# Decoder step on one core: key, mask and value steps of the sample attention moved into the projections

## The reference

```python
hn = _rmsnorm(x, g_pre_mix)
xl, gate, q, k, v, qi, ki, wi = _split_proj(hn @ w_in)
# rope on q, k, qi, ki
lru, hT, new_buf = _rglru(xl, conv_buf, h0, ...)        # conv, gates, linear recurrence
att = attend(q, k, v, qi, ki, wi)
mix = concat([lru * gelu(gate), att]) @ w_out
x = x + _rmsnorm(mix, g_post_mix)
f = square(relu(_rmsnorm(x, g_pre_ffn) @ w_ff1)) @ w_ff2
x = x + _rmsnorm(f, g_post_ffn)
```

```python
sc = _index_scores(qi, wi, ki_all)                       # admissible keys only
_, idx = lax.top_k(sc, kk)
s = einsum('...thd,...tkhd->...thk', q, kg) * HEAD_DIM ** -0.5
o = einsum('...thk,...tkhd->...thd', softmax(s), vg)
```

## Time and profile before

| | us |
|---|---|
| median of 3 runs | 909.92 |
| profiled execution | 904.44 |
| its span | 902.2 |
| TensorE busy | 821.2 |
| VectorE / ScalarE / GpSimd busy | 393.9 / 347.7 / 178.0 |

### The profile page before, as it was taken

How to read it: one execution, slowest core, us unless ns; L and a number is a source line. 1 busy time by engine, 2 the same in 40 slices (tenths; PEclk the granted TensorE clock), 3 DMA queues, 4 the chain that set the end, 5 groups by cost and what they waited for, 6 DMA issues and landing times.

```text
span 902.2 us, 16225 instructions
## 1 busy us (share of the span) xinstructions
PE 821.2 (91%) x6089; PEld 673.2 (75%) x6089; DVE 393.9 (44%) x762; ACT 347.7 (39%) x744; POOL 178.0 (20%) x173
## 2 busy tenths in 40 slices
PE   5997799899999888989996999999999999999990
PEld 4863487677865442336884899999999999999990
DVE  6129999993000342430188544322211443333327
ACT  3556455255555452422252434322222343322210
POOL 0731073433243500000023211100000111100003
PEclk9999999989999887997998999999999999999995
DMA  8421325767669869990011222222222222222202
GB/s 343 160 94 49 138 93 188 281 236 257 233 198 309 278 249 388 386 396 35 1 48 47 70 78 84 93 94 90 74 93 94 77 87 93 78 89 91 93 23 99
DMA packets 52179, 133.20 MB, mean 148 GB/s; under 512 B 6113, under 2 KB 6626, under 8 KB 50850
## 3 DMA queue, kind: packets, MB, share of 16 engines
q1 hardware_dynamic: 49442, 113.08, 36.1%
q10 hardware_dynamic: 864, 10.58, 3.3%
q0 software_dynamic: 1824, 8.86, 2.5%
HBM read 127.84 MB, written 4.67 MB: 147 GB/s over the span
## 4 chain that ended last, share of the span: by engine, by line
PE 76%; DVE 6%; DMA 6%; SPq 4%; ACT 3%; issue 3%; POOL 1%; DVEq 0%; ACTq 0%
PE bank L1571 41%; PE bank L1277 21%; SPq L372 3%; PE bank L1388 3%; PE bank L1426 3%; DMA arena<-in_ck 2%; DMA arena<-in_cv 2%; DMA wring<-in_cv 1%; PE bank L1476 1%; PE bank L1263 1%; PE bank L1400 1%; DVE scp L1015 1%; PE bank L1360 1%; DVE lx L951 1%; DVE lx L1195 1%
## 5 line engine op out<-in xcount | busy, mean ns | idle before, releaser
L1277 PE MATMUL bank<-regR,wring 128*128 128x272 f32 x640 | 155.6, 404 | 6.4 <-ACT lx L585 3.2
L1277 PEld LDWEIGHTS bank<-regR,wring 128*128 128x128 f32 x640 | 124.1, 195 | 34.9 <-issue 5.3
L1205 DVE TENSOR_TENSOR h_lo<-lx,h_hi 128x544 f32 (+1 forms) x32 | 35.8, 1120 | 111.0 <-ACT h_hi L865 110.8
L535 POOL TENSOR_TENSOR lx<-lx 128x544 f32<-128x544 f32 x30 | 32.8, 1093 | 244.6 <-ACT lx L860 244.6
L1571 PE MATMUL bank<-h_lo,w_hi_odd 128*128 128x272 f32 x256 | 73.9, 289 | 0.0
L1571 PE MATMUL bank<-h_hi,w_hi_even 128*128 128x272 f32 x256 | 73.8, 288 | 0.0
L1571 PE MATMUL bank<-h_lo,w_hi_even 128*128 128x272 f32 x256 | 73.7, 288 | 0.0
L1571 PE MATMUL bank<-h_hi,w_hi_odd 128*128 128x272 f32 x256 | 73.7, 288 | 0.0
L1571 PE MATMUL bank<-h_hi,w_lo_odd 128*128 128x272 f32 x256 | 73.6, 287 | 0.0
L1571 PE MATMUL bank<-h_hi,w_lo_even 128*128 128x272 f32 x256 | 73.5, 287 | 0.0
L1571 PE MATMUL bank<-hn_lo,w_hi_odd 128*128 128x272 f32 x240 | 69.3, 289 | 0.0
(11 more groups left out here) (267 smaller groups left out, 1711.2 us busy)
## 6 DMA issues: line engine op xcount, KB each, us to landing
arena<-in_ck SPq DMA_DIRECT2D x128, 256.0 KB, 3.8
wring<-in_w_mlp SPq DMA_DIRECT2D x64, 512.0 KB, 3.4
arena<-in_cv SPq DMA_DIRECT2D x80, 256.0 KB, 6.3
wring<-in_cv SPq DMA_DIRECT2D x48, 256.0 KB, 6.4
wring<-in_w_in ACTq DMA_DIRECT2D x4, 2048.0 KB, 8.5
wring<-in_w_in SPq DMA_DIRECT2D x2, 2048.0 KB, 12.9
regX<-in_xT SPq DMA_DIRECT2D x4, 544.0 KB, 5.5
regX<-in_xT POOLq DMA_DIRECT2D x1, 2176.0 KB, 11.6
```

What stands on the lines that cost most here:

```text
L535: nc.gpsimd.tensor_tensor(square_t[:, s, :], relu_t[:, s, :], relu_t[:, s, :], ALU.mult).then_inc(h_sq, 1)
L1205: vec.tensor_tensor(h_lo[:, at], square_t[:, parity, :], h_hi[:, at].bitcast(F32), ALU.subtract).then_inc(h_lo_rd, 1)
L1277: ins = pe.matmul(bank[e % 4][0:parts, 0:HALF], lhs(k), rhs[:, k, hf * HALF:(hf + 1) * HALF], start=(k == 0), stop=(k == KT - 1))
```

## The change

- `K_UNIT = 4`: four key steps stand behind each of the four tiles of k and of xl, none behind gate and v. The ring of key pages keeps its three slots.
- The new keys' scores and the ten mask products stand among the halves of the gate tiles, as do the first five groups of transposes; the others, and 14 value steps (`MID_VALUES`), stand among the v tiles. The remaining 18 value steps stand in the loop over prompt units, one in each second turn.
- Banks 4 and 5 take the mask products, the sample's transposes and value sums; the prompt's scores go to banks 2 and 3.
- The transposed numerators get other homes (the place of the indexer queries, of the index scores and of `kw_diag`), since regR still holds the normed input. Values have three slots (`V_SLOTS`), not five, and the first weight slot is free earlier: its output block is loaded by ScalarE behind the last gate tile.
- VectorE makes the masks before the scans of blocks 1 to 3.

```diff
-V_SLOTS = 5
+V_SLOTS = 3
+K_UNIT = 4
+MID_VALUES = 14
...
-            for s in range(3, V_SLOTS):
-                values(s, s, gemm_mm, E_V)
             for s in (30, 31):
                 keys(s, (s + 2) % 3, k_mm, s - 2)
             for s in range(3):
                 values(s, s, k_mm, KSTEPS - 2 + s)
-            with eng.Fori(0, 5) as i:
+            with eng.Fori(0, 9) as i:
...
-                for i in range(2):
-                    key_scores(8 + 2 * unit + i)
+                if unit < 4:
+                    for i in range(K_UNIT):
+                        key_scores(16 + K_UNIT * unit + i)
+                if between:
+                    between()
...
+            for j in range(2):
+                value_tile(j)
+                sample_transposes(5 + 2 * j)
+                value_products(3 * j)
+                sample_transposes(6 + 2 * j)
+                value_products(3 * j + 1)
+                value_products(3 * j + 2)
...
-            for u in range(KSTEPS + 5):
+            for u in range(ATT_UNITS + 5):
                 if u < ATT_UNITS and u % 2 == 0:
                     att_scores(u // 2)
-                if u < 10:
-                    sample_transposes(u)
...
-                if u >= 5:
-                    value_products(u - 5)
+                if u % 2 == 1 and MID_VALUES + u // 2 < KSTEPS:
+                    value_products(MID_VALUES + u // 2)
```

More of the change, by code:

```diff
@@ L1110, in _ @@
                 vec.tensor_scalar(sstat[:, g, 6:7], sstat[:, g, 5:6], -1.0, None, ALU.mult).then_inc(smax_rd, 1)
+            for c in range(1, CT):
+                scan(c)
             def masked(u):
@@ L1401, in lru_gate, with unit_end @@
                           start=True, stop=True).then_inc(lg_mm, 1)
-            def unit_end(unit):
+            def unit_end(unit, between=None):
                 gates = unit >= 0 and unit % 3 == 1
@@ L1432, in _, with new_key_scores @@
-            for g in range(GRP):
-                eng.wait_ge(k_ev, KSTEPS)
[L1434 to L1450, removed]
+            def new_key_scores():
+                eng.wait_ge(rope_out, 13)
+                eng.wait_ge(k_ev, KSTEPS)
+                for g in range(GRP):
+                    for m in range(CT):
+                        for b4 in range(4):
+                            ins = pe.matmul(bank[4 + g][32 * b4:32 * b4 + 32, 0:NS], qbd[:, 4 * g + b4, m, :], kT[:, m, SEQ:NT],
+                                            start=(m == 0), stop=(m == CT - 1))
+                    ins.then_inc(kn_mm, 1)
@@ new lines, in sample_mask @@
+            def sample_mask(n):
+                g, c = n // 5, n % 5
+                cols = slice(c * 512, min((c + 1) * 512, NKEY))
+                if n == 0:
+                    eng.wait_ge(smask_rd, 1)
+                    eng.wait_ge(kn_ev, GRP)
+                elif n >= 2:
+                    eng.wait_ge(sm_ev, n - 1)
+                rows = slice(NS * min(c, 3), NS * min(c, 3) + NS)
+                taken = smask[rows, 0:CHUNK] if c < 4 else smask[rows, CHUNK:ROW]
+                pe.matmul(bank[4 + n % 2][:, 0:cols.stop - cols.start], ind_r[rows, g, :], taken, start=True, stop=True).then_inc(sm_mm, 1)
@@ L1481, in value_products, with gate_product @@
                                         start=False, stop=True)
                 ins.then_inc(v_mm, 1)
+            w = weights(4)
+            def gate_product(m, hf):
+                product(E_GATE + 2 * m + hf, hf, lambda k: w[:, k, m * P:(m + 1) * P], hnT)
+            gate_product(0, 0)
+            new_key_scores()
+            gate_product(0, 1)
+            sample_mask(0)
+            sample_mask(1)
+            unit_end(4)
+            for m in range(1, 3):
+                for hf in range(2):
+                    gate_product(m, hf)
+                    for n in range(4 * m - 2 + 2 * hf, 4 * m + 2 * hf):
+                        sample_mask(n)
@@ new lines, in _, with value_tile @@
+            for hf in range(2):
+                gate_product(3, hf)
+                sample_transposes(2 * hf)
+                sample_transposes(2 * hf + 1)
+            unit_end(7)
+            sample_transposes(4)
+            w = weights(5)
+            def value_tile(j):
+                n = P if j < 4 else NS
+                e = E_V + j
+                slot_free(e)
+                for k in range(KT):
+                    ins = pe.matmul(bank[e % 4][0:n, :], hnT[:, k, j * P:j * P + n], w[:, k, :], start=(k == 0), stop=(k == KT - 1))
+                ins.then_inc(gemm_mm, 1)
@@ L1485, in att_scores @@
+            value_tile(3)
+            for s in range(9, 12):
+                value_products(s)
+            value_tile(4)
+            for s in range(12, MID_VALUES):
+                value_products(s)
             def att_scores(w_):
```

116 lines of the change are left out of this document (64 added, 52 removed).

## The result

The changed kernel took **949.4 us** (median of 4 runs, 945.6 to 951.9) against 910.4 for the kernel before on the same chip: ratio 1.044, 95% interval 1.041 to 1.047, slower. The profiled execution took 945.6 us where that of before took 904.4, so the two traces compared here lie 41.2 us apart. The forecast was 940 us, range 922 to 958.

What follows compares the result with a forecast made beforehand. TensorE was taken to bound the kernel, with 36.6 us recoverable. The terms -36.6 + 36 + 16 + 4.8 + 2.2 + 2 + 6 gave +30 us, which on the median of 909.9 made 940 us, range 922 to 958.

Steps and rivals of the forecast that it cites:

- The key wait: Key stage: the fourth key step of each of eight units waits 4.5 us for its slot's refill, +36 us.
- the gate block's 4.8: Key stage: the gate weight block's load, issued behind the last k unit, delays key refills, +4.8 us, between 0 and 10.
- The clock, +16: Key stage: TensorE's clock drops after each unit's wait, 2 us per unit, +16 us, bounds 0 and 23.
- The short-gap row: Trace before: no half clock followed a 2.21 us gap; by this no unit pays for the clock, sum +14 us.
- POOL and the first prompt unit, +2.2 + 2: TensorE's waits for POOL's sums before the recurrence gates, +2.2 us; first prompt unit's chain without sample work, +2 us.
- Attention, +6: Attention's start: three value slots, an output block and the v store cost +6 us, bounds 0 and 18.
- Two of the signs named in the prediction: Attention stage in the profile after: about 63 us instead of 97, and few waits for in_cv.
- The rival of the starving value ring: Attention: three slots hold up most of 18 value steps by 1 us, clock another 3 to 8; 955 to 960 us, 9%.
- -36.6: Five stages from key to attention: 36.6 us of TensorE idle time and lower clock, assumed recovered in full.

Runs made afterwards that it cites:

- keys_alone: The kernel before with only the key part: four key steps behind each k and xl tile, none behind gate and v; 955.5 us, ratio 1.050.
- halves: The changed kernel with two of the four key steps behind each half tile, in seven of eight units; 920.5 us, ratio 1.013.
- four_key_slots: The changed kernel with a fourth slot for key pages, order unchanged; 916.1 us, ratio 1.008.
- loads_late: The changed kernel with x reloaded after 30 of 32 value steps, block 6 loaded behind prompt unit 24, POOL's mix before the v store; 939.7 us, ratio 1.034.
- mix_first: The changed kernel with only POOL's four mix products moved, ahead of the v store; 949.1 us, ratio 1.044.
- x_early: The changed kernel with only the reload of x moved, issued from POOL's recurrence at 351 us instead of 380; 949.1 us, ratio 1.042.

## Why the prediction was right, and where it missed

- **Right in sign and range, and in the mechanism of the key part.** That part alone makes the kernel slower (`keys_alone`), by the wait for a refill of a three-slot ring, and a fourth slot or an even order takes most of it away. That the sum came within 10 us is luck in part: the key waits came out 5 us under their terms, and attention some 13 over its own.
- **The key wait, 4.5 us in each unit, with the gate block +36 + 4.8.** Measured 35.6 us of idle time in the key stage, 31.6 of it in waits for pages; by unit 3.9 to 5.2 us. The x branch ended at 275.5 us, forecast near 275. Of the gate block's 4.8 hardly 1 was added, since its wait took the place of the one that the unit had anyway. It became visible only where the other waits were gone (5.83 in `halves`, 8.10 in `four_key_slots`). One detail was off: that unit waits ahead of its second step.
- **The clock, +16.** 15.3 us in the key stage and 2.1 behind it by the clock column. The rule cited in the prediction from the Trainium skill ("TensorE: Matmul & The Clock Gate", section "HAM oscillation — how this bites in real kernels") has every unit pay; the trace agrees, there is half clock with the waits of all eight. The short-gap row, by which none would, did not decide.
- **POOL and the first prompt unit, +2.2 + 2.** The gate stage stands for 2.8 us. The first prompt unit's transposes wait 2.88 us for VectorE's normalising (L1142, at 379.31), which lies in attention's 16.7; the last section says what held it. Small and about right in size.
- **Attention, +6: the term that was mis-sized.** With the first prompt unit's wait the stage lost 16.7 us of idle time and 4.3 of clock, 21.0 where +6 and +2 stood. I had counted "an output block and the store of v", 3.1 MB. The reload of x, 2176 KB, comes into the same stretch since the change lets it go 8 us behind the v store, and I left it out; `loads_late` shows that moving it and the block behind the stretch takes 7 us off the stage and 10 off the median. I had also hidden a quarter of the transfers behind the slack, and given this stage no price for the clock, which added a quarter as much as the waits. Two of the signs named in the prediction failed with this term: attention took 77.75 us, not about 63, and its waits for in_cv come to 12.6 us.
- **The rival of the starving value ring.** It put 18 us in place of the 6 and 3 to 8 of clock on top. Without the first prompt unit's wait attention lost 18.1, nearer to that than to the 6. But its pattern is not the one that came: one long wait beside other transfers, and none for values from 392 us on, where it had most of the 18 steps held up. What `loads_late` leaves, 8.5 us of idle time with three slots, may be the ring's part; that stays open.

With the measured terms the sum is -36.6 + 35.6 + 17.4 + 2.8 + 0.2 + 21.0 = +40.4; the stages moved by 41.9, and most of the rest is the product's error in the key stage.

## What to carry to other kernels

Before moving a loading step into a stage, count the steps per unit against the slots of its ring: one step more in a row than the ring has slots exposed most of a refill in each unit here, though the engines could load faster, and spreading the steps over half tiles took most of that back. When a stage that loads is short of transfers, list every transfer that any queue issues in it, those that stand behind a store too, and those that the change itself lets go earlier. Moving one earlier into another loading stage only moved the loss; behind the crowded stretch it cost less.

## What I had not expected of the hardware

A VectorE operation that takes 0.29 us took 4.67 us at attention's start, and ended when the last of POOL's four mix products ended. First VectorE's rows, then POOL's, both of the change; POOL's small copies between are left out:

```profile
374.58 4.67 DVE L1142 TENSOR_SCALAR arena<-arena,stat 128x128 f32<-128x128 f32 x1
...
379.57 0.29 DVE L1142 TENSOR_SCALAR arena<-arena,stat 128x128 f32<-128x128 f32 x1
```

```profile
373.56 1.35 POOL L500 TENSOR_TENSOR regM<-regM,arena 128x544 f32<-128x544 f32 x1
...
375.11 1.34 POOL L500 TENSOR_TENSOR regM<-regM,arena 128x544 f32<-128x544 f32 x1
...
376.67 1.13 POOL L500 TENSOR_TENSOR regM<-regM,arena 128x544 f32<-128x544 f32 x1
...
378.03 1.13 POOL L500 TENSOR_TENSOR regM<-regM,arena 128x544 f32<-128x544 f32 x1
```

In `mix_first`, where these products end before the operation begins, while the transfers stay, the same line takes 0.29 us:

```profile
377.03 0.29 DVE L1143 TENSOR_SCALAR arena<-arena,stat 128x128 f32<-128x128 f32 x1
```

So POOL's products held it, not the transfers. (`x_early`, where they stand in their old place, has 4.78 us.) The Trainium skill says in "SBUF — State Buffer", section "Who interferes with whom", that VectorE operations in a two-port mode, which tensor_scalar can enter, contend with GpSimd for a port pair, and that the one which issues second is blocked until the other's instruction ends. The trace agrees that it is blocked; but it was issued in the first product, which ended at 374.91, and was held through the next three as well, to 379.25.
